# Second attention of a two-block transformer kernel: heads in pairs, column halves, and PSUM banks by use

## The chip, the core and the metric

The kernel runs on one core of a Trainium2 chip as a single launch. The metric is the device time in microseconds of that launch; the kernel before has a median of 3574.91 us over 3 runs (3573.5 to 3575.41).

## What is computed

Two transformer blocks on a sequence of S = 1024 tokens and D = 1024 channels, in float32. The first block (sparse attention, a state-space scan and a feed-forward part) is not touched. The second block, cut to what matters here, is:

```python
def mla_branch(...):      # 8 latent heads, query/key width 96, value width 64
    sc = einsum('bqhd,bkhd->bhqk', qblk, k) * scale     # causal
    p = softmax(sc);  return einsum('bhqk,bkhd->bqhd', p, v)
def diff_branch(...):     # 4 differential heads, 2 maps each of width 32, value width 64
    sc = einsum('bqhmd,bkhmd->bhmqk', qblk, k) * scale  # causal, m = 0, 1
    p = softmax(sc)
    a = p[:, :, 0] - lam * p[:, :, 1]
    o = einsum('bhqk,bkhd->bqhd', a, v);  return rms_norm(o, subln_g) * (1 - lam_init)
def mem_branch(...):      # 4 memory heads of width 64 over 256 memory tokens, not causal
    p = softmax(einsum('bshd,bmhd->bhsm', q, k) / sqrt(64))
    return einsum('bhsm,bmhd->bshd', p, v)
y = concatenate([y_mla, y_diff, y_mem]) * silu(z);  x = x + y @ w_out
```

## The kernel before, in words

Everything is laid in 128-row tiles: 8 query blocks of 128 tokens, and for query block i the keys of blocks 0 to i. Five engines run programs of their own that are written out by hand, in lockstep by a step number s; they meet through semaphores, and each engine works its instructions in the order in which they are written. The second attention is one loop of steps over a list of units, `subs2`. A unit is one map of one head and one query block: 64 units of latent heads ("m"), 64 of differential maps ("d"; the two maps of a head and block follow each other) and 8 of memory heads ("e", four query blocks at a time). For a unit of nk key blocks:

- TensorE (helper `mm`, L625) multiplies queries by keys into one or two PSUM banks: the score block. Each float32 matmul shows in the profile as two passes, so 512 columns are two MATMUL records.
- VectorE (L2207) reads the scores, adds the causal mask and takes the row minimum in one instruction, writing to a buffer `probs2`; that frees the bank.
- ScalarE (L1651, L1643) takes the exponential with its row sum.
- VectorE multiplies by the reciprocal (L2225, L2227); for a differential head it scales the second map by lambda over its sum (L2230, L2232) and adds the first map times its reciprocal (SCALAR_TENSOR_TENSOR, L1684).
- TensorE transposes the probabilities by 128-column blocks (helper `tr`, L629), four to a bank (`four`), five steps after the scores (`T_LAG`).
- ScalarE copies them from PSUM to `pT2` (L1292).
- TensorE multiplies V by them, 512 query columns at once (a "sweep" of four query blocks), seven steps after (`PV_LAG`). The stationary tile is V of two heads, 128 columns wide, and of the 128 output partitions only the 64 of the head are used. VectorE writes them out (L1681, L2243).

In the differential heads the transposes and the V products fall in every other step, so that the second map of query block i and the first map of block i+1 are issued next to each other, with nothing between them. There are 6 `probs2` buffers for latent and 8 for the other units. PSUM banks are handed out in a circle over all 8 by `bank`; each use of a bank waits until the one before was read.

VectorE's step s is: the minimum of unit s, then the scaling of unit s-2, then the V product that is done. GpSimd has nothing in these steps but splitting two tiles of the output projection's weights (`split_weights`, L1175 and L1177) and two small powers for the differential heads' norm (L1166). After the loop (`end_phase`, then `phase_done`) comes the output projection.

The diff touches these functions:

## Time and profile before

| what | value |
|---|---|
| median of 3 runs | 3574.91 us |
| the profiled execution's own time | 3577.13 us |
| its span, first to last instruction | 3575.2 us |
| latent heads' scores start | 3083 us |
| first score block on 32 rows (differential) | 3238.7 us |
| first score block on 64 rows (memory) | 3410.7 us |
| VectorE has written the last V product | 3474.0 us |

The profile shows one execution. The page lists busy time by engine (PE is TensorE's matmuls, PEld its weight loads, DVE VectorE, ACT ScalarE, POOL GpSimd), the granted TensorE clock by slices, the chain of work that ended last, and the groups of instructions; further views are cut out by time. A row of windows is the stretch and its length; the busy time (and instructions) of PE, PEld, DVE, ACT and POOL; the mean granted clock (1.00 is 2.4 GHz, 0.50 is 1.2 GHz); the DMA engines' share and GB/s. Of a group the mean duration of one instruction is given in ns. A matmul's end is modelled and takes in its way through the array, so durations of neighbouring matmuls overlap; the distance between two starts is what one costs in a row.

### The profile page before, as it was taken

The numbers are of one execution on the slowest core, as the hardware profiler recorded it, in microseconds if no ns is written. First come the engines' busy times: TensorE is split into PE (matmuls) and PEld (weight loads), VectorE is DVE, ScalarE is ACT, GpSimd is POOL, SyncE is SP. The second block draws the span as 40 slices with busy tenths as digits, with TensorE's granted clock in tenths as the row PEclk, the third lists the DMA queues.
The fourth block names the chain that finished last, engine by engine and source line by source line (L and its number), as shares of the span: only waits on it lengthen the run. The fifth ranks groups of instructions, "written<-read, shape, count | busy, mean of one in ns | idle before, by whom it ended". The sixth has DMA issues, their size and how long they took to land.

```text
span 3575.2 us, 36793 instructions
## 1 busy us (share of the span) xinstructions
PE 3283.7 (92%) x14026; PEld 2485.9 (70%) x14026; DVE 1841.7 (52%) x3008; ACT 971.4 (27%) x1810; POOL 901.1 (25%) x566
## 2 busy tenths in 40 slices
PE   7999999878779998989999999998997998899898
PEld 4577788555557886668887788887866886555467
DVE  1599991566664447871331544443334326756551
ACT  2420111355552003560001100001214114654340
POOL 0132332000002324653332433332233352100002
PEclk9899999898989999999999999999998999998679
DMA  8012332100001110112332111112112110000012
GB/s 207 12 48 66 91 103 93 60 18 8 17 18 42 48 41 34 44 48 95 102 133 89 36 52 49 47 48 100 61 53 78 48 47 15 1 1 12 0 50 81
DMA packets 185861, 196.37 MB, mean 55 GB/s; under 512 B 12257, under 2 KB 152029, under 8 KB 184029
## 3 DMA queue, kind: packets, MB, share of 16 engines
q1 hardware_dynamic: 170669, 142.08, 13.6%
q10 hardware_dynamic: 15024, 51.98, 3.9%
q8 instruction: 114, 1.87, 0.2%
q14 instruction: 54, 0.44, 0.0%
HBM read 153.15 MB, written 40.89 MB: 54 GB/s over the span
## 4 chain that ended last, share of the span: by engine, by line
PE 69%; DVE 9%; issue 9%; ACT 4%; POOL 4%; DMA 2%; DVEq 2%; POOLq 1%; ACTq 1%; SPq 0%
PE psum L625 66%; PE psum L629 3%; DVE arena L1681 3%; DVE arena L1684 2%; DVE rounded L1681 1%; ACT arena L1292 1%; POOL stat L1166 1%; POOL arena L1220 1%; DVE arena L1832 1%; DMA arena<-z_d 1%; POOL rounded L1177 1%; ACT arena L1402 1%; POOL arena L1237 1%; DVE arena L2207 1%; ACTq L1298 0%
## 5 line engine op out<-in xcount | busy, mean ns | idle before, releaser
L625 PE MATMUL psum<-rounded,rounded 128*128 128x512 f32 (+2 forms) x9504 | 2200.6, 392 | 85.1 <-DVE rounded L1681 44.8
L625 PEld LDWEIGHTS psum<-rounded,rounded 128*128 128x128 f32 x9504 | 1799.7, 191 | 458.0 <-issue 89.0
L625 PE MATMUL psum<-arena 128*128 128x512 f32 (+15 forms) x2450 | 778.9, 494 | 38.3 <-ACT arena L1292 15.5
L1175 POOL CAST rounded<-arena 128x1024 fp32r<-128x1024 f32 (+1 forms) x190 | 205.9, 1084 | 1738.2 <-DMA arena<-in_w_in 826.3
L625 PEld LDWEIGHTS psum<-arena 128*128 128x128 f32 (+4 forms) x2450 | 408.2, 205 | 334.2 <-issue 269.1
L1292 ACT ACTIVATE arena<-psum 128x512 f32<-128x512 f32 (+9 forms) x572 | 307.2, 566 | 754.4 <-PE psum L625 707.3
L1177 POOL TENSOR_TENSOR rounded<-arena,rounded 128x1024 fp32r<-128x1024 f32 (+1 forms) x190 | 466.6, 2456 | 28.2 <-issue 1.3
L629 PE MATMUL psum<-ident,arena 128*128 128x128 f32 (+1 forms) x1816 | 303.6, 313 | 150.4 <-ACT arena L1292 48.7
L629 PEld LDWEIGHTS psum<-ident,arena 128*128 128x128 f32 (+1 forms) x1816 | 242.6, 159 | 239.9 <-issue 92.0
L1681 DVE TENSOR_TENSOR arena<-arena,psum 128x512 f32<-128x512 f32 (+1 forms) x176 | 125.8, 733 | 355.2 <-PE psum L625 335.4
L1681 DVE TENSOR_TENSOR rounded<-arena,rounded 128x1024 fp32r<-128x1024 f32 (+1 forms) x132 | 198.2, 1532 | 210.8 <-ACT rounded L1295 210.2
L1295 ACT ACTIVATE rounded<-arena 128x1024 fp32r<-128x1024 f32 x116 | 117.1, 1051 | 389.9 <-PE psum L625 182.9
L1166 POOL TENSOR_TENSOR stat<-stat,neghalf 128x1 f32<-128x1 f32 (+4 forms) x65 | 97.1, 1502 | 484.6 <-DVE stat L1689 484.6
L1684 DVE SCALAR_TENSOR_TENSOR arena<-psum,cols,arena 128x1023 f32<-128x1023 f32 (+1 forms) x160 | 205.0, 1281 | 10.7 <-issue 0.4
L1992 DVE TENSOR_SCALAR arena<-psum,cols 128x1024 f32<-128x1024 f32 x44 | 59.1, 1344 | 271.6 <-PE psum L625 271.6
L1762 DVE MATCH_REPLACE8 arena<-arena 128x384 f32<-128x384 f32 (+2 forms) x192 | 165.8, 876 | 0.0
L2207 DVE CUSTOM_DVE_ANT_0 arena<-psum,strip 128x256 f32<-128x256 f32 (+7 forms) x128 | 95.8, 754 | 128.1 <-PE psum L625 127.1
L1759 DVE MAX8 arena<-arena 128x8 f32<-128x384 f32 (+2 forms) x192 | 155.5, 879 | 10.6 <-issue 10.6
L1681 DVE TENSOR_TENSOR arena<-arena 128x1024 f32<-128x1024 f32 (+3 forms) x114 | 85.1, 764 | 131.1 <-ACT arena L1292 124.3
L1402 ACT ACTIVATE arena<-arena,negmax 128x128 f32<-128x128 f32 (+7 forms) x128 | 99.1, 774 | 172.7 <-DVE negmax L1832 172.1
L1517 ACT ACTIVATE arena<-arena 128x1024 f32<-128x1024 f32 x22 | 23.4, 1062 | 450.2 <-DVE arena L1684 450.2
L1651 ACT ACTIVATE arena<-arena,negmax 128x256 f32<-128x256 f32 (+7 forms) x128 | 99.1, 774 | 166.6 <-DVE negmax L2207 165.6
(137 smaller groups left out, 1505.0 us busy)
## 6 DMA issues: line engine op xcount, KB each, us to landing
arena<-in_w_in SPq DMA_DIRECT2D x84, 512.0 KB, 3.8
arena<-in_w_ffn_up SPq DMA_DIRECT2D x44, 512.0 KB, 3.8
arena<-in_w_ffn_down SPq DMA_DIRECT2D x22, 512.0 KB, 3.6
z_d<-arena ACTq DMA_DIRECT2D x32, 256.0 KB, 3.0
gate_d<-arena ACTq DMA_DIRECT2D x16, 512.0 KB, 3.9
arena<-in_w_ssm_out SPq DMA_DIRECT2D x16, 512.0 KB, 4.0
arena<-z_d SPq DMA_DIRECT2D x8, 1024.0 KB, 4.8
arena<-gate_d ACTq DMA_DIRECT2D x16, 512.0 KB, 3.3
```

What stands on the lines that cost most here:

```text
L625: return pe.matmul(out, lhsT, rhs, start=start, stop=stop)
L629: return pe.transpose(out, src, ident[0:n, 0:n])
L1166: pool.tensor_tensor(out=v, in0=v, in1=neghalf[:, 0:1].broadcast_to(list(v.shape)), op=ALU.pow).then_inc(rstd_ready, 1)
L1175: pool.tensor_copy(high_part, raw)
L1177: pool.tensor_tensor(out=low_part, in0=raw, in1=high_part.bitcast(F32), op=ALU.subtract).then_inc(weights_split, 1)
L1292: act.activation(out, src, func, scale=scale).then_inc(empty(name), 1)
L1402: act.activation(p, p, ACT.Exp, scale=-1.0, bias=negmax[:, s % 4:s % 4 + 1], accum_out=rsum[:, s % 8:s % 8 + 1]).then_inc(exp_ready, 1)
L1681: return dve.tensor_tensor(out=out, in0=a, in1=b, op=op)
L1684: return dve.scalar_tensor_tensor(out=out, in0=a, scalar=scalar, in1=b, op0=op0, op1=op1)
L1759: dve.max(top8[:, n, :], sc)
L1762: dve.match_replace(sc, top8[:, n, :], sc, TAKEN)
L2207: dve.tensor_tensor_reduce(out=probs2[probs_slot(s)][:, 0:w], in0=psum_of(name)[:, 0:w], in1=u["mask"], scale=1.0, scalar=3e38, op0=ALU.ad ...
```

## The change

It replaces the list `subs2` by `units2`. A unit is now

- "m": two latent heads and one query block (32 units); both maps' probabilities are transposed;
- "d": the two maps of one differential head and one query block (32 units; the two heads of a pair alternate); their difference is transposed;
- "e": two memory heads and two query blocks (8 units).

Scores of the two maps of a unit are issued alternately, chunk by chunk, into different banks: banks 0 to 3 are for scores (two banks per unit, in turn, up to four key blocks; all four banks above that), 4 to 6 for transposes in turn, 7 for V products. A V product covers two query blocks (256 columns), and the two heads of the pair are two matmuls with 64 stationary columns each, one written to partitions 0 to 63 and the other to 64 to 127. There are two pairs of `probs2` buffers for latent units and four for the others.

The order of each engine's step s changes too:

- TensorE, latent units: scores s, transposes s-2, V product s-3. From the first differential unit on: transposes s-3, V product s-4, then scores s.
- ScalarE: copies of the transposes first, then the exponentials of unit s.
- VectorE: the V product that is done; then the reciprocals of unit s-1 (and its scaling for m; for e the first head's); then the two masked minima of unit s; last, for d, the addition of the two maps of unit s-2.
- GpSimd takes over the scaling of the second map of d (by lambda over its sum) and of the second memory head. Its weight split for the output projection moves behind all of these and behind the second norm's power.

```diff
+        units2 = []
+        for j in range(MLAH // 2):
+            for i in range(TT):
+                units2.append(dict(
+                    ph="m", j=j, i=i, nk=i + 1, lanes=(0, 1), sums=True,
+                    q=[qTm[0:MQK, 2 * j + m, i * P:(i + 1) * P] for m in range(2)],
+                    k=lambda m, lo, hi, j=j: kTm[0:MQK, 2 * j + m, lo:hi],
+                    v=lambda m, b, j=j: vM[:, b, (2 * j + m) * 64:(2 * j + m) * 64 + 64]))
...
+        def lag2(n):
+            return 2 if n < N_MLA else 3
+        turned_at = {n + lag2(n): n for n in range(N2)}
+        summed_at = {n + lag2(n) + 1: n for n, u in enumerate(units2) if u["i"] % 2 and u["sums"]}
...
+        def scores2_bank(n):
+            return (0, 4) if units2[n]["nk"] > 4 else (2 * (n % 2), 2)
...
 # TensorE
+            def scores2(n):
+                u, name = units2[n], ("S2", n)
+                place, banks = scores2_bank(n)
+                bank(name, banks, place)
+                for k in range(banks):
+                    pe.wait_ge(*vacated(name, k))
...
+                    for lo, hi in chunks(u["nk"] * P):
+                        for m in range(2):
+                            last = mm(out[:, m, lo:hi], u["q"][m], u["k"](m, lo, hi))
+                last.then_inc(full(name), 1)
...
+                if s < N_MLA:
+                    scores2(s)
                 if s in turned_at:
...
+                        pe.wait_ge(probs2_ready, turned_probs[n] - len(u["lanes"]) + u["lanes"].index(m) + 1)
+                        for grp in range(last_group(u) + 1):
+                            four(("T2", n, m, grp), [...], 4 + turns % 3)
+                            turns += 1
                 if s in summed_at:
...
+                    for b in range(u["nk"]):
+                        lo = P if b == u["i"] and u["ph"] != "e" else 0
+                        for m in range(2):
+                            last = mm(out[64 * m:64 * m + 64, lo:256], u["v"](m, b), at(pT2_at(u, m, b) + lo / Kf, 256 - lo),
+                                      b == 0, b == u["nk"] - 1)
                     last.then_inc(full(name), 1)
+                if N_MLA <= s < N2:
+                    scores2(s)
...
 # GpSimd
+            for n in range(N_MLA, N2):
+                if n == N_MLA + 24:
+                    power(("sub", 0))
+                u, c = units2[n], 2 * n
+                pool.wait_ge(sums2_ready, n + 1)
+                if u["ph"] == "d":
+                    p1 = probs_of(n)[1][:, 0:u["nk"] * P]
+                    pool.tensor_scalar(p1, p1, rinv[:, c % 8 + 1:c % 8 + 2], lam[:, 4:5], ALU.mult, ALU.mult).then_inc(second_scaled, 1)
...
+            power(("sub", 1))
             split_weights(*[(("o2", 0), k) for k in (0, 2)])
-            power(("sub", 0), ("sub", 1))
...
 # VectorE, after the V product of the step
+                if 1 <= s <= N2:
+                    n = s - 1
+                    u, c = units2[n], 2 * n
+                    dve.wait_ge(exp2_ready, n + 1)
...
+                        dve.reciprocal(rinv[:, c % 8:c % 8 + 2], rsum[:, c % 8:c % 8 + 2]).then_inc(sums2_ready, 1)
+                    if u["ph"] == "m":
+                        dve.drain()
+                        for m in range(2):
+                            p = probs_of(n)[m][:, 0:u["nk"] * P]
+                            dve.tensor_scalar(p, p, rinv[:, (c + m) % 8:(c + m) % 8 + 1], None, ALU.mult).then_inc(probs2_ready, 1)
+                if s < N2:
...
+                            ins = dve.tensor_tensor_reduce(
+                                out=probs_of(s)[m][:, 0:w], in0=scores2_of(s)[:, m, 0:w], in1=strip[:, (7 - u["i"]) * P:S],
+                                scale=1.0, scalar=3e38, op0=ALU.add, op1=ALU.min, accum_out=negmax[:, c % 4:c % 4 + 1])
+                            ins.then_inc(maximum2 if m == 0 else empty(name), 1)
+                if 2 <= s <= N2 + 1 and units2[s - 2]["ph"] == "d":
...
+                    dve.wait_ge(second_scaled, n - N_MLA + 1)
+                    stt(p1, p0, rinv[:, c % 8:c % 8 + 1], p1, ALU.mult, ALU.add).then_inc(probs2_ready, 1)
```

## Rows read from the trace of the kernel before

**Rows 1.** The page, part 1: busy time and share of the span by engine.
```profile
PE 3283.7 (92%) x14026; PEld 2485.9 (70%) x14026; DVE 1841.7 (52%) x3008; ACT 971.4 (27%) x1810; POOL 901.1 (25%) x566
```

**Rows 2.** Windows: latent heads, differential heads, memory heads with the tail.
```profile
3083.00:3238.70 155.70, 148.32 (x618) 90.27 (x616) 90.29 (x262) 87.12 (x213) 0.00 (x0) 0.99 0.00 1
3238.70:3410.70 172.00, 155.18 (x476) 80.27 (x474) 102.60 (x240) 74.52 (x181) 10.07 (x5) 0.70 0.02 7
3410.70:3474.00 63.30, 60.45 (x222) 40.76 (x221) 36.12 (x49) 29.28 (x89) 2.90 (x1) 0.75 0.00 0
```

**Rows 3.** Chain of waits, latent heads: start, length, engine and tile, instructions.
```profile
3210.56 7.33 PE psum L625 x20
...
3231.21 7.33 PE psum L625 x20
```

**Rows 4.** Chain of waits, late differential and memory heads.
```profile
3439.05 1.90 PE psum L629 x8
...
3452.01 0.87 PE psum L629 x8
```

**Rows 5.** Timeline of TensorE in the differential heads: start, length, tile, instructions.
```profile
3306.41 0.42 PE L629 MATMUL psum<-ident,arena 128*128 128x128 f32 x1
3306.76 3.79 PE L625 MATMUL psum<-arena 32*128 32x512 f32 x8
```

**Rows 6.** The same view, two V products of the differential heads.
```profile
3329.26 8.35 PE L625 MATMUL psum<-arena 128*128 128x512 f32 x18
...
3380.17 4.85 PE L625 MATMUL psum<-arena 128*128 128x512 f32 x6
```

**Rows 7.** Windows with one clock level each.
```profile
3305.90:3316.10 10.20, 10.20 (x27) 5.30 (x26) 7.04 (x14) 5.52 (x11) 0.00 (x0) 0.50 0.01 2
3333.20:3340.00 6.80, 6.70 (x24) 3.44 (x22) 1.77 (x5) 0.81 (x2) 0.00 (x0) 1.00 0.00 0
```

**Rows 8.** Groups by line and shape, differential heads (busy us, mean ns | idle before).
```profile
L2207 DVE CUSTOM_DVE_ANT_0 arena<-psum,strip 128x1024 f32<-128x1024 f32 x8 | 9.8, 1221 | 15.3 <-PE psum L625 15.3
...
L1651 ACT ACTIVATE arena<-arena,negmax 128x1024 f32<-128x1024 f32 x8 | 9.2, 1149 | 22.2 <-DVE negmax L2207 22.2
...
L1684 DVE SCALAR_TENSOR_TENSOR arena<-arena,rinv 128x1024 f32<-128x1024 f32 x3 | 3.9, 1284 | 0.2
...
L2207 DVE CUSTOM_DVE_ANT_0 arena<-psum,strip 128x128 f32<-128x128 f32 x8 | 2.1, 280 | 0.0
...
L1684 DVE SCALAR_TENSOR_TENSOR arena<-arena,rinv 128x128 f32<-128x128 f32 x4 | 1.4, 352 | 0.3
```

**Rows 9.** Groups by line and shape, latent heads.
```profile
L1292 ACT ACTIVATE arena<-psum 128x512 f32<-128x512 f32 x42 | 23.6, 579 | 0.0
...
L2227 DVE TENSOR_SCALAR arena<-arena,rinv 128x1024 f32<-128x1024 f32 x7 | 5.3, 753 | 0.5
```

**Rows 10.** Groups by line and shape, memory heads.
```profile
L1643 ACT ACTIVATE arena<-psum,stat 128x256 f32<-128x256 f32 x32 | 14.7, 473 | 12.8 <-DVE stat L2202 12.8
...
L2202 DVE TENSOR_REDUCE stat<-psum 128x4 f32<-128x1024 f32 x8 | 9.8, 1223 | 16.8 <-PE psum L625 16.8
```

**Rows 11.** GpSimd's groups from the differential heads to the end.
```profile
L1177 POOL TENSOR_TENSOR rounded<-arena,rounded 128x1024 fp32r<-128x1024 f32 x8 | 19.3, 2414 | 1.5 <-issue 0.4
L1175 POOL CAST rounded<-arena 128x1024 fp32r<-128x1024 f32 x8 | 8.5, 1064 | 231.1 <-DMA arena<-in_w_out 231.1
L1166 POOL TENSOR_TENSOR stat<-stat,neghalf 128x16 f32<-128x16 f32 x2 | 5.8, 2896 | 188.5 <-DVE stat L1689 188.5
```

**Rows 12.** Timeline, latent heads: end of a score block and who starts.
```profile
3217.70 0.49 PE L629 MATMUL psum<-ident,arena 128*128 128x128 f32 x3
...
3217.91 1.22 DVE L2207 CUSTOM_DVE_ANT_0 arena<-psum,strip 128x1024 f32<-128x1024 f32 x1 [5.72 <-PE psum L625]
```

**Rows 13.** Timeline, differential heads: VectorE hands over to TensorE.
```profile
3374.66 1.28 DVE L1684 SCALAR_TENSOR_TENSOR arena<-arena,rinv 128x1024 f32<-128x1024 f32 x1
...
3376.00 1.33 PE L629 MATMUL psum<-ident,arena 128*128 128x128 f32 x5 [1.12 <-DVE arena L1684]
```

More of the change, by code:

```diff
@@ L1 @@
+import itertools
 import math
@@ L154, in hybrid_two_blocks, with bank @@
         tile_of, before = {}, {}
-        def bank(name, n=1):
-            b = turn[0] if turn[0] + n <= 8 else 0
+        def bank(name, n=1, place=None):
+            b = place if place is not None else turn[0] if turn[0] + n <= 8 else 0
             turn[0] = (b + n) % 8
@@ L566, in hybrid_two_blocks @@
-        for h in range(MEMH):
-            for i in (3, 7):
-                r, j = 64 * (h % 2), h // 2
-                subs2.append(unit(
-                    "e", i, 2 * 4, [pB[r:r + 64, i - 3 + n, 768 + j * P:768 + (j + 1) * P] for n in range(4)],
-                    kmT[r:r + 64, j, :],
-                    lambda b, h=h: memkv[:, b, 256 + (h // 2) * P:256 + (h // 2 + 1) * P], h=h, four=len(subs2) % 3))
-        def first_map(u):
-            return u["ph"] == "d" and u["m"] % 2 == 0
+                units2.append(dict(
[3 more added lines that the diff above has]
+                    v=lambda m, b, j=j: vM[:, b, (2 * j + m) * 64:(2 * j + m) * 64 + 64]))
@@ L629, in tr, with four @@
                 return pe.transpose(out, src, ident[0:n, 0:n])
-            def four(name, blocks):
-                out = bank(name)
+            def four(name, blocks, place=None):
+                out = bank(name, 1, place)
                 pe.wait_ge(*vacated(name))
@@ L1055, in _ @@
                 if s in summed_at:
                     n = summed_at[s]
-                    u, name = subs2[n], sweep_of(subs2[n])
-                    first = 4 * (u["i"] // 4)
-                    pT = pT2[u["i"] // 4]
-                    pe.wait_ge(*written(("T", N1 + n, last_group(u))))
-                    out = bank(name)
-                    pe.wait_ge(*vacated(name))
-                    keys = 2 if u["ph"] == "e" else u["nk"]
-                    for b in range(keys):
-                        lo = max(0, b - first) * P if u["ph"] != "e" else 0
-                        last = mm(out[:, lo:512], u["v"](b), pT[:, b, lo:512], b == 0, b == keys - 1)
+                    u, name = units2[n], summed(n)
@@ L1070, in _ @@
                         pe.wait_ge(sub_squared, j + 1)
-                        out = bank(("ss", j))
+                        out = bank(("ss", j), 1, 7)
                         pe.wait_ge(*vacated(("ss", j)))
@@ L1075, in _ @@
                         last.then_inc(full(("ss", j)), 1)
-                    if s == pair_end[j] + 8:
+                    if s == pair_end[j] + 6:
                         pe.wait_ge(sub_spread, j + 1)
                         for half in range(2):
-                            four(("sr", j, half), [rs_wide[:, j, 4 * half + n, :] for n in range(4)])
+                            four(("sr", j, half), [rs_wide[:, j, 4 * half + n, :] for n in range(4)], 4 + turns % 3)
+                            turns += 1
             end_phase(pe)
@@ new lines, in _ @@
+                    if same_area(n) is not None:
+                        act.wait_ge(*completed(same_area(n)))
+                    here = slice((u["i"] % 2) * P, (u["i"] % 2 + 1) * P)
+                    for m in u["lanes"]:
+                        for grp in range(last_group(u) + 1):
+                            name = ("T2", n, m, grp)
+                            if u["ph"] == "e":
+                                copy(at(pT2_at(u, m, 0), 512), name)
+                                continue
+                            w = min(4, u["nk"] - 4 * grp)
+                            copy(at(pT2_at(u, m, 4 * grp), 4, 256)[:, 0:w, here], name,
+                                 psum_of(name)[:, 0:w * P].rearrange("p (a b) -> p a b", b=P))
@@ L2235, in _ @@
[L2235 to L2245 removed]
+                    o = psum_of(name)[:, 0:256]
```

273 lines of the change are left out of this document (137 added, 136 removed).

## The prediction

> **What bounds the kernel now.** I read the page first: TensorE is busy for 92% of the span, VectorE for 52% [rows 1]. Then the windows, cut where the scores change their rows [rows 2]. The second attention takes 155.7 + 172.0 + 63.3 = 391.0 us, and everything outside it stays. In the latent heads TensorE is busy for 148.3 of 155.7 us at clock 0.99; in the differential heads for 155.2 of 172.0 at 0.70; in the memory heads for 60.5 of 63.3 at 0.75. Elsewhere VectorE is busy for 90.3, 102.6 and 36.1 us. So TensorE sets the pace, and in two of the three stretches its clock does too.
>
> What work costs on it: from one V product to the next the chain of waits has 20.65 us, one latent head [rows 3]. Its 7.33 us with 20 passes are a V product of 2 x 3328 columns and four score passes of 512, 8704 columns, so 0.43 us per pass of 512 at the high level, 0.86 us per float32 matmul of 512 columns. Eight transposes take 0.87 us there and 1.90 at the low level [rows 4]. A head's triangle has 36 blocks of 128: scores 7.7 us, transposes 3.9, V product (4608 columns too) 7.7, all at full clock.
>
> **Two heads at a time on the array.** The change pairs heads on the array, so the question is what overlaps already. At clock 0.50 the V product at 3380.17 has six passes in 4.85 us [rows 6], some 0.85 for each of 512 (the sixth runs on). Eight passes on 32 rows (widths 896 and 1024, two maps) take 3.79 us [rows 5], at clock 0.50 too [rows 7], where one after another they would need 3840 x 2 / 1024 x 0.85 = 6.4. So the maps on neighbouring row groups already run together: the second map of block i with the first of block i+1, which the program issues next to each other. Alternate issue in the differential heads only evens out widths: a pair costs its wider map now, 43 blocks per head against 36, 1.5 us per head. It is no factor of two.
>
> New are the column halves. A V product of two heads costs 15.4 us now and 7.7 if the halves run together: 30.7 us for four latent pairs, 15.4 for two differential ones, 7 for memory, at full clock. No row shows two column halves at once. Bounds: full overlap (nothing more to pay) and none (the 53 us are not saved). I take overlap, as row groups do it.
>
> Changing from 128 rows to 32 costs: the last transpose starts at 3306.41, the scores at 3306.76 instead of 3306.62, and their four slots of 0.85 take 3.79 and not 3.41 [rows 5]. That is 0.5 us per change to and fro; I charge V products in halves 0.4 as well. The Trainium skill (TensorEngine Tiling, Key Properties) says that every change of the tiling mode drains TensorE, which speaks against the halves; the trace agrees with 0.5 us for row groups, and if the 32 V products paid nothing, as the rule excludes, the sum would be some 8 us lower. The Trainium skill also gives 2.38 times for three column tiles (TensorE: Matmul & The Clock Gate, Part 3); by that factor's efficiency of 0.79 the V products would save some 15 us less, an estimate from that page that no row here shows.
>
> **What the new order waits for.** The hand-overs first: a minimum starts 0.2 us after its scores' last column has gone in [rows 12], a transpose 0.06 us after the addition ends [rows 13].
>
> *Differential heads.* TensorE's step is now transposes s-3, V product s-4, scores s. The transposes s-3 need the addition s-3, which VectorE does last in its step s-1, behind the two minima of unit s-1, which need the scores s-1. So everything is one ring: scores, two minima, addition, transposes, (V product), scores. Before, the transposes lagged five steps, so that at least one addition was in stock and TensorE and VectorE worked side by side. Exponentials (two of 1.15) and GpSimd's scaling hang beside the ring with two steps of room. Its price per head, over eight units: minima from 0.28 to 1.22 us, about linear in width, so 2 x 8 x 0.75 = 12.0; additions from 0.35 to 1.28, 8 x 0.82 = 6.5 [rows 8]; hand-overs and changes 0.76 each, 6.1. Then TensorE's scores of both maps 7.7, transposes 3.9 and V product 3.8, divided by the clock c. Four heads, with 3 us for the norm: 101 + 62/c. At c = 1 that is 163 us, at the 0.70 of before 190, at 0.50 225, against 172 now. So the ring costs more than it saves unless the clock rises above 0.87.
>
> *The clock.* It stood at 0.50 through stretches in which TensorE was busy without a gap but with 32-row scores for most of it, as with 3305.9 to 3316.1, and at 1.00 in 3333.2 to 3340.0 [rows 7], once the V product on 128 rows that began at 3329.26 had run for 4 us [rows 6]. In the ring TensorE also stands still while VectorE works (18.5 of some 50 us per head), and V products are half as long. I take 0.60, between the low level and 0.70: 204 us, 32 more than now.
>
> GpSimd's scaling of 1024 columns is in no row: between its cast, 1.06 us, and its product, 2.41 [rows 11]. Either fits into the two steps of over 8 us, so it costs nothing; at small widths it is an eighth of that.
>
> *Latent heads.* Per pair TensorE has 15.4 + 7.9 + 7.7 = 31 us, with eight changes 32.6, 130 for four pairs. But above four key blocks the scores take all four banks: the next scores wait for both minima. Steps of 5 to 8 blocks then cost scores 11.1 + minima 8.2 (pairs of 0.82, 0.95, 1.09 and 1.22) + 0.3 each = 20.5, with transposes and small V products hidden in the minima. Steps of 1 to 4 blocks: scores 4.3, transposes of the large units 3.9, V products 5.5, changes 0.8: 14.5. Sum 35.0, 140 us: the lower bound. The second chain: minimum s follows the scaling of s-1 (0.75 each [rows 9]), which follows both exponentials of s-1, which follow ScalarE's copies of the transposes s-2 (four of 0.58 with 0.1 overlap [rows 9]), and these follow the scores s-1. Laid out on the eight steps with these durations, the score blocks of a pair begin at 0, 4.9, 7.5, 12.6, 16.2, 20.5, 25.6 and 32.0 us and the next pair at 38.7: 155 us. If no copy is in time it is 158. I take 154, 2 less than now.
>
> *Memory heads.* Ring: four exponentials (0.47 and a sum's read, 0.58 start to start), drain 0.1, reciprocal and drain 0.24, the first head's two scalings 0.7, reduction 1.22 [rows 10], hand-overs 0.2: 4.9 us, 39 for eight units. TensorE's 2.6 us per unit lie beside it (scores 0.86, eight transposes 0.87, V product 0.86; before 4.3, since scores and V product cost twice that). To it come the last differential units' drain, 7 us, and the end: GpSimd starts its power (2.90) and both weight splits (1.06 + 2.41 each) only after its last scaling, so 0.8 + 2.9 + 6.9 = 10.6 us, longer than the V product's way out (5). Sum 57 against 63, 6 less; 50 if warm throughout, 65 if low. Before, the splits lay at 3260 to 3268 beside the differential heads.
>
> The sum: 154 + 204 + 57 = 415 against 391.0, +24 us. The execution profiled has 3577.1 us with a span of 3575.2, the median is 3574.9: 3599 us.
>
> **The rivals.**
> 1. *The ring decides* (above), 3599. Own range 3583 to 3625: c from 0.70 to 0.50, less 4 in the latent heads at the lower end.
> 2. *The clock stays high, faster.* Both maps on the array together and V products on all 128 columns keep it up; the ring's TensorE part shrinks. c = 1: 163 + 154 + 52 = 369, -22, 3553 us. Deciding point: c = 0.80, where 101 + 62/c is 178 and the sum 391. Against it: a busy TensorE was at 0.50 with two maps together, and now it pauses.
> 3. *Column halves don't overlap.* 53 us of work come back, 15.4 of it at c 0.6 (26): 31 + 26 + 7 = 64, 3663 us. For it: no row. Against it: row groups do.
> 4. *The ring and the bank wait hide more than I think*: latent heads at 140 and c at 0.75 (184 us): 381, -10; at c 0.70, 387, 3571 us, no change to be told.
>
> **How the numbers follow.** Chances: 0.64 for 1, 0.12 for 2, 0.11 for 3, 0.13 for 4. A measurement tells 0.2%, 7 us, from no change: faster is below 3568, slower above 3582. Rival 4 lies half in the same and a quarter each side. Faster 0.12 + 0.03 = 0.15; same 0.06 and 0.05 of case 1's lower end, 0.11; slower the rest, 0.74. The range takes in case 1, 4 and the near part of 2 (c up to 0.92), 3560, and stops short of 3: 3640.
>
> **What would show it.** Differential heads: transposes that wait for the addition, two minima right behind each other after a wait for the scores, TensorE and VectorE busy by turns, clock 0.5 to 0.65, 190 to 225 us. V products: two passes of 256 columns with starts a few ns apart, 0.43 us per key block; if 0.86, rival 3. Latent heads: above four blocks scores that wait for VectorE. Memory heads: TensorE idle for a third. I am wrong if the windows show the differential heads under 178 us, or the latent heads under 140.

## The result, and the profile after

The kernel after takes 3607.1 us (median of 4 runs, 3603.0 to 3612.8) against 3574.7 us of the kernel before on the same chip. The ratio is 1.0092, with a 95% interval of 1.0075 to 1.011: 0.9% slower. Predicted were 3599 us, 3560 to 3640. One execution of the kernel before (4259.6 us) and one of V head by head below (4801.9 us) ran at a granted clock of 0.73 and 0.64 and are left out of the ratios, and the latter of its median. The profiled execution took 3605.1 us with a span of 3603.3, 28.1 us more than before's.

Windows of the kernel after, cut as [rows 2] were: at the first 96-row, 32-row and 64-row scores. The last one here reaches on to the output projection's first matmul.

```profile
3080.00:3245.90 165.90, 138.23 (x752) 86.16 (x752) 86.32 (x238) 89.55 (x222) 0.00 (x0) 0.95 0.00 1
3245.90:3440.80 194.90, 128.75 (x522) 68.28 (x520) 78.53 (x206) 74.34 (x176) 29.12 (x33) 0.59 0.02 6
3440.80:3505.10 64.30, 44.09 (x265) 29.72 (x264) 29.43 (x52) 30.54 (x90) 25.49 (x22) 0.77 0.03 9
```

TensorE has less to do everywhere: 138.2, 128.8 and 44.1 us busy where it had 148.3, 155.2 and 60.5. Yet the latent heads take 10 us more and the differential heads 23 more. TensorE was busy for 90% of the differential heads before and is for 66% now, and the clock granted there fell from 0.70 to 0.59. Only the memory heads gain: to the output projection's first matmul they took 66.4 us before and take 64.4.

Who waits for whom in the differential heads after (total us, times, longest):

```profile
DVE arena L2327 <- PE psum L654: 108.2, 32, 8.0
ACT arena L1734 <- DVE negmax L2327: 99.5, 31, 7.4
PEld psum L658 <- DVE arena L1753: 88.7, 29, 5.1
PE psum L658 <- DVE arena L1753: 65.4, 29, 3.5
```

L654 is a matmul, L658 a transpose, L2327 the masked minimum, L1753 the addition of the two maps. VectorE waits for the scores once in each of the 32 units, 108 of 195 us, and the transposes wait for the addition in 29 of them. The chain of waits shows one unit after another going round:

```profile
3315.94 1.54 PE psum L658 x6
3317.48 3.74 PE psum L654 x8
3321.22 0.02 issue
3321.24 1.22 DVE arena L2327
3322.48 1.14 DVE arena L2327
3323.62 1.07 DVE arena L1753
3324.70 0.04 issue
3324.74 1.75 PE psum L658 x7
```

From one unit's transposes to the next one's it is 8.8 us, of which TensorE has 5.3 and VectorE 3.4, by turns.

The V product in column halves, in TensorE's timeline of the latent heads (eight key blocks, two heads):

```profile
3126.24 3.46 PE L654 MATMUL psum<-arena 128*64 128x256 f32 x32
```

32 passes, of which 28 have 256 columns and four 128, take 3.46 us with their way through the array. One after another at full clock they would take 7680 / 512 x 0.43 = 6.5. The halves run together.

### The profile page after: what moved, and what is told of

Its sections match the earlier page's. It is cut to its first block, busy times and chain, and to the rows that moved or that the text cites. A ratio compares the mean times of both kernels' runs of the same rounds, so it can differ in the third digit from the quotient of the medians.

```text
span 3603.3 us, 37089 instructions
## 1 busy us (share of the span) xinstructions
PE 3223.2 (89%) x14250; PEld 2453.3 (68%) x14250; DVE 1806.3 (50%) x2952; ACT 971.9 (27%) x1810; POOL 942.8 (26%) x614
## 4 chain that ended last, share of the span: by engine, by line
PE 66%; DVE 12%; issue 9%; ACT 5%; POOL 4%; DMA 2%; DVEq 1%; POOLq 1%; ACTq 1%; SPq 0%
PE psum L654 63%; PE psum L658 3%; DVE arena L1750 3%; DVE arena L1753 2%; DVE arena L2327 2%; DVE rounded L1750 2%; ACT arena L1353 1%; POOL stat L1214 1%; DVE arena L1901 1%; POOL arena L1268 1%; DMA arena<-z_d 1%; POOL rounded L1225 1%; ACT arena L1463 1%; POOL arena L1285 1%; DVE arena L1911 1%
## 5 line engine op out<-in xcount | busy, mean ns | idle before, releaser
L654 PE MATMUL psum<-rounded,rounded 128*128 128x512 f32 (+2 forms) x9504 | 2196.0, 392 | 86.1 <-DVE rounded L1750 45.9
L654 PEld LDWEIGHTS psum<-rounded,rounded 128*128 128x128 f32 x9504 | 1795.5, 190 | 458.5 <-issue 89.0
L654 PE MATMUL psum<-arena 128*128 128x512 f32 (+17 forms) x2674 | 716.5, 479 | 65.0 <-DVE negmax L2327 24.0
L654 PEld LDWEIGHTS psum<-arena 128*128 128x128 f32 (+5 forms) x2674 | 384.5, 197 | 342.2 <-issue 256.9
L658 PE MATMUL psum<-ident,arena 128*128 128x128 f32 (+1 forms) x1816 | 303.9, 315 | 213.7 <-DVE arena L1753 70.5
L658 PEld LDWEIGHTS psum<-ident,arena 128*128 128x128 f32 (+1 forms) x1816 | 243.9, 161 | 294.9 <-DVE arena L1753 95.2
L1753 DVE SCALAR_TENSOR_TENSOR arena<-psum,cols,arena 128x1023 f32<-128x1023 f32 (+1 forms) x160 | 205.0, 1281 | 10.7 <-issue 0.4
L2327 DVE CUSTOM_DVE_ANT_0 arena<-psum,strip 128x128 f32<-128x128 f32 (+7 forms) x128 | 92.1, 755 | 147.1 <-PE psum L654 112.4
L1828 DVE MAX8 arena<-arena 128x8 f32<-128x384 f32 (+2 forms) x192 | 155.5, 879 | 10.6 <-issue 10.6
L1463 ACT ACTIVATE arena<-arena,negmax 128x128 f32<-128x128 f32 (+7 forms) x128 | 99.1, 774 | 171.4 <-DVE negmax L1901 170.8
L1734 ACT ACTIVATE arena<-arena,negmax 128x128 f32<-128x128 f32 (+7 forms) x128 | 98.3, 770 | 107.2 <-DVE negmax L2327 106.6
```

Of the source, the lines that this page charges most:

```text
L654: return pe.matmul(out, lhsT, rhs, start=start, stop=stop)
L658: return pe.transpose(out, src, ident[0:n, 0:n])
L1463: act.activation(p, p, ACT.Exp, scale=-1.0, bias=negmax[:, s % 4:s % 4 + 1], accum_out=rsum[:, s % 8:s % 8 + 1]).then_inc(exp_ready, 1)
L1753: return dve.scalar_tensor_tensor(out=out, in0=a, scalar=scalar, in1=b, op0=op0, op1=op1)
L1828: dve.max(top8[:, n, :], sc)
L2327: ins = dve.tensor_tensor_reduce(out=probs_of(s)[m][:, 0:w], in0=scores2_of(s)[:, m, 0:w], in1=strip[:, (7 - u["i"]) * P:S], scale=1.0, sc ...
```

## The experiments

All were run against the kernel before on the same chip. The stretches are those of one profiled execution each, in us: latent, differential, and memory to the output projection's first matmul. What lies ahead of the second attention is the same in all, but its start varies from 3071 to 3085 us between executions; so a stretch tells more exactly than the whole time what an edit did. A stretch has a scatter of its own: the latent heads, whose instructions are the same in after, addition first and scaling on VectorE, took 165.6, 166.3 and 166.5 us. Where the scores come first, the first 32-row scores are issued ahead of the last latent transposes and V product, so 38 of TensorE's latent passes, 4 to 6 us, move into the differential stretch. The runs were made in groups on different chips, in which before's medians were 3574.1, 3572.4 and 3574.5 us; medians of different groups compare no better than to 2 us.

| kernel | median | ratio (95%) | latent | diff. | memory |
|---|---|---|---|---|---|
| before | 3574.7 | 1 | 156.3 | 171.9 | 66.4 |
| after | 3607.1 | 1.0092 (1.0075 to 1.011) | 165.6 | 194.9 | 64.4 |
| addition first | 3549.9 | 0.9929 (0.9903 to 0.9956) | 166.3 | 144.1 | 60.7 |
| scores first | 3524.6 | 0.987 (0.9833 to 0.9907) | 159.3 | 133.2 | 54.3 |
| both orders | 3531.9 | 0.9874 (0.9847 to 0.9902) | 161.8 | 134.3 | 56.9 |
| V on full columns | 3645.3 | 1.0198 (1.0172 to 1.0225) | 191.1 | 210.1 | 71.5 |
| V head by head | 3638.8 | 1.0172 (1.0145 to 1.0198) | 188.1 | 208.6 | 66.1 |
| scores map by map | 3602.5 | 1.0082 (1.0064 to 1.01) | 168.0 | 195.2 | 62.0 |
| scaling on VectorE | 3622.1 | 1.0133 (1.0114 to 1.0152) | 166.5 | 215.2 | 64.8 |
| late scaling | 3594.2 | 1.0057 (1.0038 to 1.0076) | 160.6 | 195.9 | 62.0 |
| banks by head | 3585.1 | 1.0032 (1.0017 to 1.0047) | 148.9 | 194.3 | 64.4 |
| scores first, GpSimd's order | 3527.2 | 0.9866 (0.9835 to 0.9897) | 161.8 | 136.8 | 50.4 |
| four edits | 3498.7 | 0.9786 (0.9759 to 0.9814) | 141.2 | 140.3 | 44.0 |
| four without late scaling | 3505.3 | 0.9803 (0.9778 to 0.9828) | 143.1 | 138.3 | 50.5 |

### Is it the ring? Two ways to open it

Addition first: on VectorE the addition of unit s-2 moves ahead of the minima of unit s.

```diff
+                if 2 <= s <= N2 + 1 and units2[s - 2]["ph"] == "d":
+                    ...   # the addition, word for word
                 if s < N2:
                     ...   # minima of unit s
-                if 2 <= s <= N2 + 1 and units2[s - 2]["ph"] == "d":
-                    ...
```

> Only VectorE's order is changed: the addition of unit s-2 comes before the two minima of unit s instead of behind them. Ring theory: the transposes no longer wait for the newest scores; the additions (6.5 us per head) and the transposes (3.9 at full clock, some 6.5 at the clock measured) leave the ring and lie beside TensorE's and VectorE's other work, 4 x (6.5 + 6.5) = 52 us less in the differential heads (194.9 to some 143), the kernel at 3555, faster than before. Clock theory (the stretch is long because TensorE works at 0.59, whatever it waits for): its work there, 62 at full clock and 105 at 0.59, has to be done anyway, the order on VectorE changes little, 5 to 10 us: 3600.

Scores first: TensorE issues the scores of unit s ahead of transposes and V product in the differential and memory heads too.

```diff
-                if s < N_MLA:
+                if s < N2:
                     scores2(s)
...
-                if N_MLA <= s < N2:
-                    scores2(s)
```

> Only TensorE's order is changed: from the first differential unit on the scores of unit s come before the transposes s-3, as in the latent heads. Ring theory: the minima of s run beside the transposes and the V product, so the ring is cut at its other end: two minima and an addition per unit on VectorE (4.0 of 5 us for 8 blocks, 74 us for four heads) and 62 us at the clock on TensorE overlap; differential heads 130 to 150, memory heads some 8 less, the kernel at 3535 to 3560. Clock theory: no gain beyond 10 us. If both orders had to be changed together to gain, neither this nor the addition first would help.

Measured: 144.1 and 133.2 us in the differential heads instead of 194.9. The first hits what was expected (143 us, 3555 for the kernel, measured 3549.9); with scores first the stretch is as expected and the kernel, at 3524.6, faster than the 3535 to 3560. No work was taken out; the same minima, additions and passes stand in another order. Windows of the differential heads with addition first, then with scores first:

```profile
3248.40:3392.50 144.10, 121.80 (x524) 66.48 (x522) 77.59 (x205) 69.43 (x174) 41.62 (x32) 0.64 0.03 8
```

```profile
3234.50:3367.70 133.20, 116.24 (x551) 64.10 (x551) 79.67 (x207) 73.49 (x181) 27.95 (x32) 0.69 0.03 9
```

TensorE is busy for 85 and 87% instead of 66, and the clock rises from 0.59 to 0.64 and 0.69. VectorE's wait for scores fell from 108.2 to 39.6 us with addition first and to 22.1 with scores first:

```profile
DVE arena L2325 <- PE psum L654: 22.1, 17, 2.1
```

Are these two waits or one?

> Both new orders at once: TensorE issues the scores of a step first, and VectorE does the addition ahead of the two minima. Theory A, one ring: either order opens the same ring, and once it is open TensorE's own work at its clock and VectorE's sum (about 12.0 + 6.5 us a head plus reciprocals) run side by side, so the second order adds nothing: 3524 us (3515 to 3533), differential heads 130 to 136 us. Rival B, two separate waits: the gains of the two orders (57 and 82 us) add up: 3468 us. Rival C, the addition ahead of the minima holds up the scores' release, since it waits for GpSimd: 3535 to 3550 us.

3531.9 us and 134.3 in the differential heads, as with scores first alone: the gains don't add up. There is one ring, and either order opens it. Addition first alone stays 11 us behind scores first in the stretch; VectorE still waits 39.6 us for scores there, and what else is in those 11 us was not separated.

### What the column halves are worth

V on full columns: the stationary tile is the V of both heads, 128 columns, for each head in turn, into separate columns of the bank; the half of the output partitions that belongs to the other head is computed and not used. VectorE writes each product out in two instructions instead of one, which is part of this kernel's time too.

```diff
-                    for b in range(u["nk"]):
-                        for m in range(2):
-                            last = mm(out[64 * m:64 * m + 64, lo:256], u["v"](m, b), ...
+                    for m in range(2):
+                        for b in range(u["nk"]):
+                            last = mm(out[:, 256 * m + lo:256 * m + 256], u["v2"](b), ...
```

> The column halves undone alone: each V product of 256 columns is two runs of matmuls with all 128 stationary columns (both heads' V), into the two halves of the bank, of which half the partitions are read; VectorE writes the result out in two instructions instead of one. If the halves are worth what two overlapped matmuls save: 31 us of work in the latent heads at full clock of which the waits of the large steps hide little, since the V products of 6 and 8 blocks fall into small steps: +20 to +31; differential heads 15.4 at clock 0.6 in the ring, +20 to 26 less the dearer changes of mode (0.4 x 8 x 0.5) and less if the longer 128-row work raises the clock; memory +3 to 7. Sum +40 to +60, 3650 to 3665. If most of it hides in waits: below +20.

Measured: 38 us more than after, just short of the 40 to 60 expected, and in the stretches 25.5 + 15.2 + 7.1 = 47.8. (The profiled execution has a span 42.2 us above after's, and its latent scores start 5.6 us earlier.) So the halves do run together and are what the change gains, up to what the second write costs; the next kernel is free of that.

V head by head keeps the halves, and only changes the order in which their matmuls are issued.

```diff
-                    for b in range(u["nk"]):
-                        lo = P if b == u["i"] and u["ph"] != "e" else 0
-                        for m in range(2):
+                    for m in range(2):
+                        for b in range(u["nk"]):
+                            lo = P if b == u["i"] and u["ph"] != "e" else 0
```

> The V products are still in column halves, but all matmuls of one head's half are issued before those of the other, instead of by turns. If TensorE's queue lets a later half start as it let the second map and the next block's first map start together in the kernel before, without being issued by turns, nothing changes for short products (2 and 4 key blocks) and little for long ones: 3607, within 5 us. If the two run together only when issued by turns, the halves' gain is lost: as in the kernel with V products on all 128 columns, which took 38 us more, less its second write-out: +25 to +40.

32 us more than after, and 37.9 in the stretches (22.5 + 13.7 + 1.7): four fifths of what the halves gave is gone. Timeline of the same V product that took 3.46 us above, and under it the passes that are on their way in three pieces of it, from the windows (the first column behind the length is PE):

```profile
3131.28 6.10 PE L654 MATMUL psum<-arena 128*64 128x256 f32 x32
```

```profile
3131.20:3133.90 2.70, 2.70 (x14) 1.00 0.00 0
3133.90:3134.50 0.60, 0.60 (x8) 1.00 0.00 0
3134.50:3137.25 2.75, 2.75 (x18) 1.00 0.00 0
```

The two heads overlap for 0.6 us in the middle, where the last passes of the first and the first ones of the second are next to each other in the program.

Scores map by map does the same to the scores: all chunks of one map, then all of the other.

```diff
-                    for lo, hi in chunks(u["nk"] * P):
-                        for m in range(2):
+                    for m in range(2):
+                        for lo, hi in chunks(u["nk"] * P):
```

> The scores of the differential and memory heads are issued map after map instead of by turns; the banks are the same. By the trace of before, where the second map of a block and the first of the next ran together although issued one after the other, they should overlap all the same: 3607, within 5 us. If issue by turns is what makes them overlap, the differential heads' scores double in the ring: 4 x 7.7 / 0.6 = 51 us at the clock measured, memory heads 7 more: 3660.

Nothing changes: 195.2 us in the differential heads. Its timeline has the same eight passes in 3.79 us as [rows 5] of before:

```profile
3316.86 3.79 PE L654 MATMUL psum<-arena 32*128 32x512 f32 x8
```

So alternate issue of the maps, a part of the change, bought nothing. Four passes of a map are few enough to overlap with the next map's; the 16 of a V product are not.

### What GpSimd's help is worth

Scaling on VectorE: the second map's scaling of the differential units goes back to VectorE, right ahead of the addition.

```diff
-                    pool.tensor_scalar(p1, p1, rinv[...], lam[:, 4:5], ALU.mult, ALU.mult).then_inc(second_scaled, 1)
...
-                    dve.wait_ge(second_scaled, n - N_MLA + 1)
+                    dve.tensor_scalar(p1, p1, rinv[...], lam[:, 4:5], ALU.mult, ALU.mult)
+                    dve.drain()
                     stt(p1, p0, ...)
```

> Only the move to GpSimd is undone for the differential heads: VectorE scales the second map by lambda over its sum right before it adds the maps, as before the change; the memory heads stay. Ring theory: the scaling (0.35 to 0.81 us, 5.1 per head) with its drain (0.1 each) now stands in the ring, 4 x 5.9 = 24 us more in the differential heads, 219 for 194.9, the kernel at 3631. Rival: VectorE idles for over half of this stretch, so the work fits into its waits: within 5 us. Or GpSimd's scaling was itself late in the ring: then less than 3607.

15 us more, and 20.3 in the differential heads, where the ring gets longer by this scaling. In the kernel after, GpSimd's 29 us there cost nothing, as predicted: among the waits of the stretch there is none of VectorE for GpSimd.

### The latent heads

Late scaling: VectorE does the reciprocals and the scaling of latent unit s-1 behind the minima of unit s instead of ahead of them.

```diff
-                if 1 <= s <= N2:
+                if 1 <= s <= N2 and not units2[s - 1]["ph"] in ('m',):
...              # and behind the minima of unit s:
+                if 1 <= s <= N2 and units2[s - 1]["ph"] in ('m',):
+                    ...
```

> Latent heads only: the scaling of unit s-1 on VectorE comes behind the minima of unit s instead of before them. Theory of the prediction (second chain: exponentials, scaling, next minimum): the minima start as soon as scores and buffer allow, 1 to 2 us per pair less, 40.5 to some 39, 3 to 7 us in all. Rival, buffer theory: the minima wait for the transposes of unit s-2, since there are only two pairs of buffers, and the order of the scaling does not matter or makes the transposes later: 0, or up to 4 us more.

Banks by head: each head's scores have their own banks and signals, and the latent heads' scores are issued head after head, so that the first head's minimum starts before the second head's scores are done, and the next scores need one bank pair and not all four.

```diff
+                    outs = [bank(("S2", n, m), wide, 2 * m if wide == 2 else 2 * (n % 2) + m) for m in range(2)]
...
+                    if u["ph"] == "m":
+                        for m in range(2):
+                            ready(m)
+                            for lo, hi in chunks(u["nk"] * P):
+                                last = mm(outs[m][:, lo:hi], u["q"][m], u["k"](m, lo, hi))
+                            last.then_inc(full(("S2", n, m)), 1)
```

> Score banks are handed over map by map: the two maps' scores have each a name, a signal and a release of their own (same banks), and a latent unit's first head is issued whole before its second; its minimum can start after the first head's scores and its banks are free after the first minimum. Bank theory for the latent heads (above four blocks the next scores wait for both minima, and these for both scores): the first minimum starts half a score block earlier and the next scores one minimum earlier, 1.1 us for each of the 16 large steps and as much for the earlier minimum where it counts: latent heads 165.6 to 140 to 150. Differential heads: the ring's minima start the same, scores are by turns as before; -0 to -5. The kernel at 3585 to 3595. Rival, buffer theory: the minima wait for the transposes of unit s-2 which come behind the scores of s in TensorE's order, so an earlier signal from the scores is worth nothing: latent heads within 3 us.

Late scaling gives 5.0 us in the latent heads, banks by head 16.7, and neither moves the differential heads. (The medians fell by 12.9 and 22.0 us; the profiled execution with late scaling, 3604.8 us, was the slowest of its six.) The rival of both expectations, that only the buffers count and neither edit gives anything, fell. Windows of the latent heads with banks by head:

```profile
3071.50:3220.40 148.90, 134.78 (x752) 85.22 (x752) 86.26 (x238) 89.03 (x221) 0.00 (x0) 0.97 0.00 1
```

TensorE's idle time there is 14 us, and 28 in the kernel after. The hand-over of four banks at once, together with the shared signal and the order of issue, was half of it; the edit changes all three and doesn't tell them apart.

### Together

> Scores first and GpSimd's order alone: the splits of two weight tiles (1.06 + 2.41 us each) lie beside differential units 14 and 15, and the second power (2.9 us) comes ahead of GpSimd's last scaling. Theory: the splits stood behind the last scaling and ahead of the output projection, and the end waited for them: 5 to 8 us less than scores first alone (3524.6), 3517 to 3520 us. Rival: the chain of VectorE, TensorE and the last V product sets the end and the splits were hidden in it: 3524 us, or 3 us more where the splits hold up the second map's scaling in the differential heads.

The splits of two weight tiles beside differential units 14 and 15, and the second power ahead of GpSimd's last scaling, gained nothing that can be told as a whole (3527.2 for 3524.6 us): the end is 3.9 us shorter (50.4 for 54.3), the differential heads are 3.6 longer (136.8 for 133.2). The rival's time held, but not by its mechanism: GpSimd's scalings are not late, and beside the splits two additions of 896 columns take 1.38 and 1.34 us and not 1.15, which is 0.4 of the 3.6. The rest stays open.

> As the kernel with four edits, but without the late scaling: scores first, banks by head, GpSimd's order. 3524.6 - 22 - 5 = 3498 us; latent heads 149 us as with banks by head alone, differential heads 130 to 136. If the late scaling gives something of its own beside banks by head, this one is 5 to 13 us slower than the kernel with all four; if both relieve the same wait, the two are within 4 us.

> Four edits at once: scores first on TensorE in every step; each head's scores have banks and signals of their own in the latent and differential heads; VectorE scales latent and memory units behind the minima of the next unit; GpSimd splits the output projection's weights beside differential units 14 and 15 and makes the second norm's power ahead of its last scaling. Sum of the single gains, if each is of its own wait: from 3524.6 us (scores first) less 22 (banks by head), less 0 to 13 (late scaling), less 5 (GpSimd's order): 3484 to 3498 us. Rival: banks by head and late scaling relieve the same wait in the latent heads, then the second of them gives nothing: 3498 us.

3498.7 us: 2.1% faster than before (1.9 to 2.4 by the interval) and 3.0% faster than after; that is the time of the rival, by which two of the edits relieve one wait. Windows of it:

```profile
3071.40:3212.60 141.20, 129.76 (x714) 81.11 (x714) 81.15 (x231) 85.13 (x214) 0.00 (x0) 0.98 0.00 1
3212.60:3352.90 140.30, 121.81 (x551) 66.30 (x551) 82.40 (x212) 74.83 (x184) 34.75 (x36) 0.66 0.03 8
3352.90:3396.90 44.00, 36.26 (x273) 24.55 (x272) 28.02 (x54) 30.11 (x90) 20.95 (x18) 0.96 0.05 13
```

The second attention takes 325.5 us where it took 394.6 before and 424.9 after. Without late scaling it is 3505.3; the intervals of the two ratios overlap, so the whole times do not tell them apart. The stretches do, by place: in the latent heads late scaling is worth 1.9 us beside banks by head, not the 5.0 it had alone, so both relieve much the same wait; the 6.5 us lie in the memory heads (44.0 for 50.5), where this kernel scales late too and the single experiment did not; there VectorE's waiting for ScalarE's exponentials falls from 9.1 to 0.5 us, and the clock is 0.96 for 0.90.

## Why the prediction was right, and where a term was off

**The ring** (rival 1, 0.64) decided. Its members came in the order predicted (scores, two minima, addition, transposes), and opening it at either of two places gives back 51 to 62 us. The formula 101 + 62/c makes 206 us of the measured clock, 194.9 were measured. The chain of waits puts 33% of the stretch on VectorE, 65 us, where the working had 4 x 18.5 = 74. The instructions last as long as in [rows 8], but a second minimum starts while the first's result is still being read, and the addition likewise, which the working charged in full:

```profile
3312.84 1.09 DVE L2327 CUSTOM_DVE_ANT_0 arena<-psum,strip 128x896 f32<-128x896 f32 x1 [4.48 <-PE psum L654]
3313.86 0.08 DVE L2327 DVE_READ_ACCUMULATOR2_ANT negmax<- 128x1 f32 x1
3313.86 1.08 DVE L2327 CUSTOM_DVE_ANT_0 arena<-psum,strip 128x896 f32<-128x896 f32 x1
```

**The clock** was taken at 0.60 and stood at 0.59. The 0.60 was a choice between two values and not worked out, so that it came this close is luck; that it would lie below 0.70 was argued. One of the arguments misreads its rows: in 3305.9 to 3316.1 of before, scores on 32 rows don't fill most of the time but 3.7 us, and a V product on 128 rows 4.4:

```profile
3311.61 5.15 PE L625 MATMUL psum<-arena 128*128 128x512 f32 x10
```

(Eight of these ten passes are the V product's.) So these rows don't show that 32-row scores go with the low clock, and no run tried it. The other argument, the pauses, the runs bear out: with the ring open TensorE is busy for 87% and not 66, and the clock is 0.69, about the 0.70 of before. So the low clock in the kernel after was in part a consequence of the ring, and opening it gives more than the idle time it removes: 49 us of TensorE's idle time went (66 to 17), and the stretch got 62 shorter. Rival 2 (clock high) fell. (At its deciding point, c = 0.80, the working's own terms add up to 389 and not 391, which changes nothing.)

**Column halves** overlap, so rival 3 fell. It had priced them at 64 us; V on full columns cost 48 in the stretches (38 in the medians). In the memory heads the term was right (7 for 7.1); in the latent heads 25.5 of 30.7 and in the differential heads 15.2 of 26 came, there at clock 0.62 and not 0.59. By the working's own 62/c that is some 5 us less for the rest of TensorE's work there, about half of what is missing; why the clock rose was not tried. The change to and from the halves had been charged with 0.4 us per V product. Behind the one shown above the next scores start at 3129.64, 3.39 us after its first pass, and its columns take 3.23, so it is 0.2 us or little more at full clock. With the change taken in, 6.45 us of passes took 3.39, a factor of 1.9: the efficiency of 0.79 that the prediction weighed is not seen here. Rival 4 (more is hidden) fell as a whole, for the latent heads hid less than thought; the differential heads hid 9 us more.

**The latent heads** are the step that was mis-sized: "the next pair at 38.7", 155 us for four, 154 taken; measured were 165.6. From one pair's four-block scores to the next pair's the trace has 40.5 us once and 40.2 once. The layout left out that the minimum of unit s writes the buffer of unit s-2, and that the transposes which free it are issued behind the scores of unit s. The chain after, between scores and minima of one step:

```profile
3138.61 2.82 PE psum L654 x8
3141.43 0.45 PE psum L658 x4
...
3142.02 0.96 DVE arena L2327
```

0.45 us of transposes stand there, and in the other steps of this pair 0.24, 0.34, 0.45 and 0.67: 2.15 together, against the 1.5 to 1.8 that were missing per pair. The waits name it too:

```profile
DVE arena L2327 <- PE psum L658: 34.7, 25, 3.3
```

That this is the cause was read from the chain and not tried with a third pair of buffers. Late scaling speaks for it: with VectorE free earlier, these waits grow from 34.7 to 61.0 us. The rest, 165.6 less four times 40.2 to 40.5, is 4 to 5 us and was not taken apart; the clock was 0.50 from 3080 to 3085 us and between 0.52 and 0.60 in three more short stretches, which could make that much, where before it was 0.99 over the whole. Of the hand-overs that were counted, the one of banks and signals by pairs of heads was the dearest: 16.7 us by the experiment.

**The memory heads**: 57 us predicted to VectorE's last write, 61.4 measured. The working had 7 us of drain, seven periods of 4.9 from the first reduction to the last, and 4.9 + 10.6 behind it. Measured are 2.2, 41.3 and 17.9. In an undisturbed stretch a unit takes 4.2 us (3462.01 to 3466.26 in the chain), less than the 4.9. But the last differential units go round the ring inside the first memory units, at 6.5 us each, and not ahead of them. The chain there:

```profile
3442.97 1.23 DVE stat L2318
3444.19 1.20 DVE arena L1753
3445.40 0.04 issue
3445.44 1.97 PE psum L658 x8
3447.41 2.03 PE psum L654 x8
```

And from the seventh reduction to the eighth it is 9.8 us. Scores stand last in TensorE's step: those of the last unit are issued behind the norm's sums, eight transposes and a V product, and VectorE waits 4.4 us for them.

```profile
3474.50 1.21 DVE L2318 TENSOR_REDUCE stat<-psum 128x4 f32<-128x1024 f32 x1
...
3484.27 1.23 DVE L2318 TENSOR_REDUCE stat<-psum 128x4 f32<-128x1024 f32 x1 [4.36 <-PE psum L654]
```

The end was also set by another thing than I wrote. The splits were over at 3499.8 us, but the output projection waited until 3505.19 for what comes behind the second power:

```profile
3488.83 0.90 POOL arena L1339
3489.73 2.89 POOL stat L1214
3492.64 1.50 DVE arena L2285
...
3498.53 1.85 DVE arena L1750
...
3502.66 1.06 ACT rounded L1356
3503.82 1.24 DVE rounded L1750
...
3505.19 6.93 PE psum L654 x23
```

The power (2.89), the spread of its result (1.50), its transposes, the products with it on VectorE (1.85 is one of them) and ScalarE's and VectorE's rounding are in line behind GpSimd's last scaling. That GpSimd starts its power only after its last scaling was right. The splits behind it are not on the path themselves, but they lengthen it. They ran from 3492.57 to 3499.83, beside the spread and the product, and with GpSimd's order, where no split runs there, the same two instructions take 0.69 us each instead of 1.50 and 1.85:

```profile
3419.08 0.69 DVE L2285 COPY arena<-stat 128x1024 f32<-128x1024 f32 x1
...
3424.24 0.69 DVE L1750 TENSOR_TENSOR arena<-arena 128x512 f32<-128x512 f32 x1
```

That is 2.0 of the 3.9 us by which that kernel's end is shorter.

The terms, predicted and measured: latent 154 and 165.6, differential 204 and 194.9, memory 57 and 61.4; sum 415 and 421.9. Errors of +12, -9 and +4 us partly cancelled, so that the whole was off by only 8 us is in part luck.

## What to carry to other kernels

When two engines hand work to each other in steps, list for each step what the last instruction of one engine waits for and what the first of the other does: a lag of three steps is worth nothing when the order within the step ties it up again, and here one moved line was worth 82 us. In this kernel, work that shared the array had to be issued by turns, pass by pass, unless it was only a few passes long. A shared signal for two results makes the consumer of the first wait for the second and the owner of the banks for both: give each its own.

## What the runs showed of the hardware

**TensorE starts matmuls ahead of their turn, a few passes far.** In the kernel with scores map by map eight passes of 512 columns on 32 rows take 3.79 us at clock 0.50, where one map's four alone need 4 x 0.85 = 3.4: the second map ran beside the first, though all of the first's were issued ahead of it. In the V product head by head the overlap is only 0.6 us (32 passes in 6.10 us, where wholly by turns they take 3.46): the second head's first pass starts at 3133.93 us in the trace, when three of the first head's sixteen have not started yet. How far ahead it can be was not tried with other lengths. The Trainium skill (TensorE: Matmul & The Clock Gate, Part 3) has matmuls start and end strictly in program order; eight passes in little more than the time of four, and a second head's pass that starts before three of the first's, do not agree with that, and here the measurement decides.

**GpSimd and VectorE exclude each other in these two instructions.** With addition first, GpSimd's scaling of 1024 columns meets the addition. In the timeline:

```profile
3318.45 1.27 DVE L1753 SCALAR_TENSOR_TENSOR arena<-arena,rinv 128x1024 f32<-128x1024 f32 x1
3318.63 2.15 POOL L1335 TENSOR_SCALAR arena<-arena,rinv,lam 128x1024 f32<-128x1024 f32 x1 [5.90 <-DVE rinv L2307]
```

The scaling takes 2.15 us where the kernel after has 1.19, and ends 1.06 us after the addition, as if it had begun when that was over. With scores first it is the other way round: the scaling started first and kept its 1.19, and the addition took 2.02 and not 1.28.

```profile
3300.73 1.19 POOL L1333 TENSOR_SCALAR arena<-arena,rinv,lam 128x1024 f32<-128x1024 f32 x1 [6.48 <-DVE rinv L2305]
...
3300.98 2.02 DVE L1751 SCALAR_TENSOR_TENSOR arena<-arena,rinv 128x1024 f32<-128x1024 f32 x1
```

The Trainium skill (SBUF — State Buffer, SBUF: two separate sides) says that a VectorE instruction with two inputs from SBUF and a GpSimd instruction that reads SBUF take turns on a shared pair of ports: whichever starts first holds it for its whole length, and the other waits. Both rows agree.

**GpSimd's scaling by one scalar was slower than by two.** At 256 columns it took 0.99 us in the memory heads (one multiplication) and 0.55 in the differential heads (two), by the groups of the kernel after:

```profile
L1339 POOL TENSOR_SCALAR arena<-arena,stat 128x256 f32<-128x256 f32 x16 | 15.7, 988 | 33.2 <-DVE stat L2300 33.2
```

```profile
L1335 POOL TENSOR_SCALAR arena<-arena,rinv,lam 128x256 f32<-128x256 f32 x4 | 2.2, 554 | 17.8 <-DVE rinv L2307 17.8
```

The scalings come in twos, and VectorE's own run only beside the first (1.06 us); the second (0.91) has none beside it, so that is not the reason. Why is open; no run separated it.
